# Two-model transformer kernel: three norms' squares summed on VectorE, even attention's scores in pairs over four banks

## Time and profile before

| | |
|---|---|
| median of three runs | 2680.15 us (2676.91 to 2689.09) |
| the profiled execution | 2677.15 us, its span 2675.3 us |
| TensorE, busy share of the span | 94% |
| TensorE, weight loads | 70% |
| VectorE | 44% |
| ScalarE | 18% |
| GpSimd | 9% |
| mean granted TensorE clock | 0.982 of full |
| DMA, mean | 291 GB/s |
| chain of work that ended last | TensorE 80%, DMA 12%, VectorE 6%, ScalarE 1% |

### The profile page before, as it was taken

The page is one execution under the profiler, slowest core; times in us unless marked ns, Lnnn a source line. Parts: engine busy times, 40 slices in busy tenths (PEclk is TensorE's granted clock), DMA queues, the critical chain, the costliest instruction groups (busy, mean ns, idle before and its releaser), DMA issues.

```text
span 2675.3 us, 40698 instructions
## 1 busy us (share of the span) xinstructions
PE 2523.6 (94%) x16446; PEld 1860.0 (70%) x16446; DVE 1164.0 (44%) x2714; ACT 480.5 (18%) x1041; POOL 245.2 (9%) x280
## 2 busy tenths in 40 slices
PE   6999999989989998999999799999999999999998
PEld 3555545566667964666676456679899866798997
DVE  2355114321115653111111322668777626687776
ACT  2142003221101022010000121431200114312001
POOL 0000000000001100000011000002122100021221
PEclk9999999999999999999999899999999999999999
DMA  9868999999998768999999983424644544245440
GB/s 405 342 275 360 420 413 407 418 420 393 418 419 345 312 277 337 419 418 419 418 416 416 420 346 112 144 95 158 252 160 182 209 159 146 95 158 220 158 158 17
DMA packets 121785, 779.78 MB, mean 291 GB/s; under 512 B 13248, under 2 KB 16960, under 8 KB 37888
## 3 DMA queue, kind: packets, MB, share of 16 engines
q1 hardware_dynamic: 94976, 684.76, 63.5%
q0 software_dynamic: 22560, 82.32, 8.0%
q10 hardware_dynamic: 4064, 10.09, 1.0%
HBM read 771.35 MB, written 5.77 MB: 290 GB/s over the span
## 4 chain that ended last, share of the span: by engine, by line
PE 80%; DMA 12%; DVE 6%; ACT 1%; issue 1%; SPq 0%; ACTq 0%; DVEq 0%
PE bank L758 78%; DMA ring<-in_stream 11%; PE bank L1202 1%; DMA work<-in_stream 1%; PE bank L762 1%; DVE work L2487 1%; DVE MX L2467 1%; DVE bank L2469 0%; DVE work L2380 0%; SPq L608 0%; DVE X L2421 0%; ACT work L1892 0%; ACT work L1792 0%; DVE X L2980 0%; ACT work L1788 0%
## 5 line engine op out<-in xcount | busy, mean ns | idle before, releaser
L758 PE MATMUL bank<-A,work 128*128 128x128 f32 (+1 forms) x3152 | 547.9, 323 | 8.9 <-DMA work<-in_stream 4.5
L758 PEld LDWEIGHTS bank<-A,work 128*128 128x128 f32 x3152 | 477.8, 192 | 68.2 <-issue 31.2
L758 PE MATMUL bank<-A,ring 128*128 128x128 f32 (+1 forms) x3088 | 474.9, 303 | 10.9 <-ACT A L1902 5.8
L758 PEld LDWEIGHTS bank<-A,ring 128*128 128x128 f32 x3088 | 424.5, 193 | 42.9 <-issue 12.7
L758 PE MATMUL bank<-work 128*128 128x128 f32 (+2 forms) x2704 | 398.8, 316 | 22.4 <-ACT work L1792 8.0
L758 PE MATMUL bank<-ring,A 128*32 128x512 f32 (+3 forms) x2272 | 366.4, 611 | 32.3 <-DMA ring<-in_stream 30.6
L758 PEld LDWEIGHTS bank<-work 128*128 128x128 f32 (+1 forms) x2704 | 316.8, 175 | 81.9 <-issue 38.1
L758 PEld LDWEIGHTS bank<-ring,A 128*32 128x32 f32 (+2 forms) x2272 | 116.7, 124 | 261.1 <-issue 200.8
L758 PE MATMUL bank<-work,ring 128*128 128x128 f32 (+1 forms) x1696 | 289.5, 318 | 1.6 <-DVE work L2500 1.6
L758 PEld LDWEIGHTS bank<-work,ring 128*128 128x128 f32 x1696 | 255.9, 191 | 20.2 <-DVE work L2500 2.1
L698 POOL TENSOR_TENSOR work<-ring,work 128x512 f32<-128x512 f32 (+1 forms) x106 | 141.3, 1333 | 683.2 <-DVE work L2514 546.1
(11 more groups left out here) (344 smaller groups left out, 2006.8 us busy)
## 6 DMA issues: line engine op xcount, KB each, us to landing
ring<-in_stream SPq DMA_DIRECT2D x652, 1024.0 KB, 14.9
work<-in_stream POOLq DMA_DIRECT2D x140, 512.0 KB, 9.1
spill<-work ACTq DMA_DIRECT2D x6, 512.0 KB, 6.1
work<-in_stream POOLq DMA_DIRECT2D x8, 384.0 KB, 8.5
work<-spill POOLq DMA_DIRECT2D x6, 512.0 KB, 4.7
X<-in_xt ACTq DMA_DIRECT2D x1, 2048.0 KB, 13.3
work<-spill POOLq DMA_DIRECT2D x2, 768.0 KB, 11.8
tab_sb<-in_tab_a ACTq DMA_DIRECT2D x1, 1120.0 KB, 9.5
```

The source lines that it names most:

```text
L758: return pay(pe.matmul(o, w, x, start=start, stop=stop, tile_position=place), tells)
```

## The change

1. The squares of n2_0, n1_1 and n2_1: ScalarE writes all eight chunks into buffers of their own, with no wait for TensorE. VectorE adds them, seven additions chained by a semaphore (`add_own`), in n2_0 and n2_1 one step behind the residual additions, in n1_1 behind the expert stage. TensorE makes one product of the sum with the ones (`total_square`): for n2_0 behind the first of the three strips, for n1_1 behind a context step, for n2_1 behind the first of two router strips.
2. The even attention makes two heads' scores together, over four banks (0, 1, 2, 7). The order of the heads in memory changes so that neighbouring heads lie in different halves of the partitions: the queries' weight columns were laid out as (0,4), (1,5), (2,6), (3,7) before, and head h now reads pair h // 2, half h % 2; the rows of `w_out_even` and the sinks follow the same order.
3. Its six strips of modulation rows stand at t = 1, 2, 3, 4, 6, 8. They add up in bank 6 in place of bank 2; VectorE copies that bank inside the attention loop, at t = 10, and TensorE waits for this copy before the first value product of block 1.
4. The copy for the next group (`mod_copy(3)`) moves behind the scaling of n2_0.
5. Slot n1_1 gets one context step and slot a9 loses one. VectorE's share of slot n1_1 stands behind the second weight sums of odd_in.
6. Ahead of the second router TensorE waits for the context's `out` 5 in place of 3.

```diff
@@ CONTEXT_STEPS @@
-    "c8": 2, "d8": 3, "n1_1b": 1, "a9": 2, "b9": 2, "c9": 2, "d9": 1,
+    "c8": 2, "d8": 3, "n1_1": 1, "n1_1b": 1, "a9": 1, "b9": 2, "c9": 2, "d9": 1,
...
+ATT_MOD_AT = (1, 2, 3, 4, 6, 8)
...
+SUMMED = ("n2_0", "n1_1", "n2_1")
...
+        SQUARES = {"n2_0": wk(0, KD, T), "n1_1": wk(0, KD, T), "n2_1": wk(13312, KD, T)}
+        SQUARE_SUM = wk(16128, T)
...
-        MOD_BANK = (4, 6, 2, 5, 4, 6, 5, 4, 4, 4)
+        MOD_BANK = (4, 6, 6, 5, 4, 6, 5, 4, 4, 4)
...
-        SBANKS = {"even": (0, 1), ...
+        SBANKS = {"even": (0, 1, 2, 7), ...
@@ tensor @@
+            def total_square(name):
+
+                pe.wait_ge(own_added, (KD - 1) * (SUMMED.index(name) + 1))
+                mm(bank[6][:, 0:T], ones, SQUARE_SUM, True, True, tells=True).then_inc(own_total, 1)
...
-                    pair = 2 if name[:2] == "na" else 1
+                    pair = 1 if name[:3] == "mla" else 2
...
                             elif u0:
                                 pe.wait_ge(at_p, u0)
+                            elif i == SBANKS[name].index(7):
+                                pe.wait_ge(mod_taken, 3)
...
-                    filling = name == "even" and 1 <= t <= EVEN_OUT_MOD - ATT_MOD
-                    if filling:
-                        mod_rows(ATT_MOD + t - 1)
+                    if name == "even" and t in ATT_MOD_AT:
+                        mod_rows(ATT_MOD + ATT_MOD_AT.index(t))
...
                         pe.wait_ge(at_ptc, g + 1)
+                        if h == 1 and name == "even" and b == 1:
+                            pe.wait_ge(mod_copied, 3)
...
-                      lambda h, b: QK[64 * (h // 4):64 * (h // 4) + 64, h % 4, b * P:(b + 1) * P],
-                      lambda h: KV_K[64 * (h // 4):64 * (h // 4) + 64, :],
-                      lambda kb, h: V1[:, kb, 64 * (h // 4):64 * (h // 4) + 64],
+                      lambda h, b: QK[64 * (h % 2):64 * (h % 2) + 64, h // 2, b * P:(b + 1) * P],
+                      lambda h: KV_K[64 * (h % 2):64 * (h % 2) + 64, :],
+                      lambda kb, h: V1[:, kb, 64 * (h % 2):64 * (h % 2) + 64],
...
-            for n in range(EVEN_OUT_MOD, ROUTE_MOD[0]):
+            mod_rows(EVEN_OUT_MOD)
+            total_square("n2_0")
+            for n in range(EVEN_OUT_MOD + 1, ROUTE_MOD[0]):
                 mod_rows(n)
-            norm("n2_0", T)
...
             beside("n1_1")
-            norm("n1_1", T)
+            total_square("n1_1")
             beside("n1_1b")
...
-            norm("n2_1", T)
-            wait_ctx(pe, "out", 3)
-            route_mods(1, 0, 2)
+            wait_ctx(pe, "out", 5)
+            route_mods(1, 0, 1)
+            total_square("n2_1")
+            route_mods(1, 1, 2)
@@ scalar @@
+            def own_squares(name, come):
+
+                i = SUMMED.index(name)
+                act.activation(OPEN[:, :], EPS[:, 0:1], ACT.Sqrt)
+                for k in range(KD):
+                    come(k)
+                    act.activation(SQUARES[name][:, k, :], X[:, k, 0:T], ACT.Square).then_inc(own_square, 1)
+                act.wait_ge(own_total, i + 1)
+                act.activation(RSTD, bank[6][:, 0:T], ACT.Sqrt, bias=EPS[:, 0:1], scale=1.0 / D).then_inc(std_ready, 1)
...
-                squares(name, w, lambda k: X[:, k, 0:w], come=come)
+                own_squares(name, come)
@@ vector @@
+            def add_own(name, k):
+
+                i = SUMMED.index(name)
+                dve.wait_ge(own_square, KD * i + k + 1)
+                if k > 1:
+                    dve.wait_ge(own_added, (KD - 1) * i + k - 1)
+                dve.tensor_tensor(SQUARE_SUM, SQUARES[name][:, 0, :] if k == 1 else SQUARE_SUM, SQUARES[name][:, k, :], ALU.add)\
+                   .then_inc(own_added, 1)
...
                         normalize(t - 1)
+                    if name == "even" and t == HEADS + 2:
+                        dve.wait_ge(mod_raw, 3)
+                        mod_copy(2)
...
-            dve.wait_ge(mod_raw, 3)
-            mod_copy(2)
             take_mods(2, 0, 2, 0, 6)
...
+                for k in range(1, 3) if j == 3 else range(j - 1, j) if j > 3 else ():
+                    add_own("n2_0", k)
+            add_own("n2_0", KD - 1)
...
             norm("n2_0", T, ...
+            dve.wait_ge(mod_raw, 4)
+            mod_copy(3)
...
-            beside("n1_1")
+            for k in range(1, KD):
+                add_own("n1_1", k)
             link(gain(3, 1, 8, 0, par_("g1", KD, KD)))
             sum_weights(-1, 0)
...
             sum_weights(-1, 1)
+            beside("n1_1")
             beside("n1_1b")
...
                 residual("odd_out", j, T, MOD[:, 1, 16 + j, 0:1])
+                if j > 1:
+                    add_own("n2_1", j - 1)
+            add_own("n2_1", KD - 1)
```

More of the change, by code:

```diff
@@ L174 @@
     NBASE[_n], NSTAT[_n], NMEAN[_n], NOUT[_n], NMID[_n], NXC[_n] = _b, _s, _m, _o, _d, _x
-    _b += 0 if _n in SHIFTED else NCHUNK[_n]
+    _b += 0 if _n in SHIFTED + SUMMED else NCHUNK[_n]
     _d += 0 if _n == "final" else NCHUNK[_n]
@@ L454, in build_program @@
         odd_sums = sem("odd_sums")
+        own_square, own_added, own_total = sem("own_square"), sem("own_added"), sem("own_total")
         ffn_scalar, ffn_vector = sem("ffn_scalar"), sem("ffn_vector")
@@ L486, in build_program @@
         UNIT0 = {"na": 0, "mla0": 8, "mla1": 12}
-        SBANKS = {"even": (0, 1), "na0": (0, 1, 2, 7), "mla0": (0, 1, 2), "na1": (0, 1, 2, 7), "mla1": (0, 1, 2)}
+        SBANKS = {"even": (0, 1, 2, 7), "na0": (0, 1, 2, 7), "mla0": (0, 1, 2), "na1": (0, 1, 2, 7), "mla1": (0, 1, 2)}
         def score_bank(name, g):
@@ L2660, in _ @@
                     beside("in_d")
-            dve.wait_ge(mod_raw, 4)
-            mod_copy(3)
+                for k in range(1, 3) if j == 3 else range(j - 1, j) if j > 3 else ():
+                    add_own("n2_0", k)
+            add_own("n2_0", KD - 1)
             def over_pass(q, p, g2):
@@ L3223, in lay_out @@
                  _tm(w[:, 1280:1792]), _pad(16)])
-    put("even_out", [_fm(I["w_out_even"][0])])
+    put("even_out", [_fm(I["w_out_even"][0][np.r_[order, 512:D]])])
     for l in range(2):
@@ L3286, in lay_out @@
         p(a, _vec(I[b]))
-    p("sink", np.broadcast_to(I["attn_sink"].reshape(1, HEADS), (P, HEADS)))
+    p("sink", np.broadcast_to(I["attn_sink"].reshape(2, 4).T.reshape(1, HEADS), (P, HEADS)))
     rb = np.stack([np.concatenate([I["b_router_group"][l], I["b_router_expert"][l]]) for l in range(2)])
```

## The result

The changed kernel took 2660.26 us (median of four runs, 2658.59 to 2661.65), the kernel before 2680.82 in the same comparison; the ratio on record is 0.9931, with a 95% interval of 0.9906 to 0.9956 (the two medians alone give 0.9923). That is 20.6 us less, where 12.3 had been forecast, and inside the range given (2658 to 2676). Two later comparisons gave 18.3 us (ratio 0.9935) and 15.9 us (0.9941). Over all of the runs the medians are 2678.7 (43 runs of the kernel before, 2669.4 to 2689.1) and 2660.6 (15 runs of the changed one, 2656.9 to 2663.0): 18.1 us.

The account below looks back on a forecast made before the run. TensorE was taken to set the pace up to 208 us, the weight stream from there. Gains of 8.7 + 0 + 1.2 + 2.4 = 12.3 us against the midpoint 2678.65 gave 2666.4 us, range 2658 to 2676.

Parts of the forecast that it names:

- Attention: Even attention: paired scores and the early copy start even_out at 170.2 instead of 178.89, a gain of 8.7 us.
- The first part: Even attention up to the scores of heads 10 and 11, bound by TensorE: 27.5 us from 124.53, ending at 152.0.
- VectorE's part: Even attention from 152.0 on, bound by VectorE's tops, normalizations and copies: 14.3 us, ending at 166.3.
- the tail of 2.9 us: End of the even attention: last normalization to last value product stays 2.9 us, ending at 169.2.
- the case "1.7 more": Even attention: if the half-clock stretch, seen at the first strip, goes, 1.7 us more are gained.
- The clock rival: Rival: clock falls where VectorE bounds the attention and TensorE idles between pieces; 10.7 us lost, 2677.1; chance 0.07.
- n2_0, 0 forecast: First norm: path 4.3 us shorter, but waited out in the second unit's 18.82 us ring wait; 0 taken, ends 0 and 4.3.
- The ring wait in the second unit longer, by some 4 us: Sign, second unit of the first expert stage: the wait for the ring grows by some 4 us.
- n1_1 and a9: Second norm: TensorE goes on about 2.3 us later, a context step moved out of a9 gives 3.5; gain 1.2.
- the step is not won back: Rival in a9: that expert unit waits for its weights anyway, so +3.5 us, 2669.9; chance 0.10.
- n2_1: Third norm: one product puts the root 2.4 us earlier, and the router waits for it; gain 2.4, ends 0.7 and 4.
- Slower: Rival, first expert stage: context steps 4.3 us out of step with the stream, nine units lose 38.7, 2705.1; chance 0.05.

Follow-up runs that it names:

- n2_0 old with the late copy: The changed kernel with n2_0 as eight products again, the copy of modulation rows still behind its scaling; 2662.31 us.
- attention alone: The kernel before with only the changed kernel's even attention, all norms and context steps as before; 2666.66 us, ratio 0.9961.
- attention with n2_0: The changed kernel with n1_1, n2_1 and the context steps as before; 2664.69 us.
- the norms alone: The changed kernel with the old even attention, one head's scores at a time over two banks; 2670.88 us, ratio 0.9977.

## Why the prediction held, and where its steps failed

**Attention, 8.7 forecast, 8.5 to 10.2 measured** in the eight traces with this attention. The first part was to end at 152.0 and the next piece starts at 151.55; VectorE's part was to take 14.3 us and ends at 165.90, 14.3 later; the tail of 2.9 us and the start of even_out right behind the columns came as worked out. In the first trace the first strip took 2.85 us in place of 3.62, as only part of it ran at the lower clock. The trace in which all of it did (3.62, n2_0 old with the late copy) has the lead of 8.5, and the three in which that stretch is missing (0.97 becomes 1.00 in the window of 120 to 172 us) have 10.1 to 10.2: the case "1.7 more" of the prediction, to the tenth. The Trainium skill's "TensorEngine Tiling (Array Packing)", under PSUM Bottleneck, warns that emptying the banks may come to bound what packed products give. The trace agrees for half of it: 7.8 of VectorE's 14.4 idle microseconds went, and behind head 10 VectorE is the bound, with TensorE waiting 0.24 to 1.30 us for its normalizations.

**The clock rival** did not come true there. The pair at 154.34 took 1.13 us amid those waits, and the granted clock from 150 to 170 us is 1.00 in every trace. The rule named for it (the Trainium skill, "TensorE: Matmul & The Clock Gate", under HAM oscillation) is not borne out at this place by any trace here; its own example has a wait for DMA behind each burst of products, so this place is no full test of it. Ahead of the first router the traces lean its way: in the two where TensorE waits 2.87 and 2.86 us for a late copy, all of the router's 32 products behind it ran at the lower clock and took 7.02 us; in the twelve others they took 3.74 to 5.74.

**n2_0, 0 forecast; nothing left in the path behind the second unit, 1.8 to 2.9 us in the medians.** The value was right for the stream, and the reasoning had a hole: "the chain waits 18.82 us for the ring" was taken for room in which any gain is waited out. The room was 1.01 + 2.72 us, less than the 4.2 won. So the 0 was in part luck. Between the router and the end of the second unit the changed kernel loses 4.9 us of its lead, more than n2_0 had given: 1.65 in the new wait at 224.57, 0.8 in the two ring waits of the unit, and most of the rest to the lower clock (1.1 in the router's products, 5.19 + 3.65 us against 4.31 + 3.41, and 0.5 in the products between the ring waits, 5.34 against 4.82). In all, ring waits between 208 and 830 us, the new one included, are 12.5 us against 10.5. "The ring wait in the second unit longer, by some 4 us" was wrong: the chain's piece grew by 1.5 us and TensorE's own waits by 0.8. Behind the second unit the four traces with the new n2_0 and the same stream lead by 8.4 to 9.8 us, the four with the old one by 9.4 to 11.5. The 1.8 us between the medians of the one set that has both kernels has overlapping ranges; the 2.9 us is taken over sets (2660.6 and 2663.5).

**n1_1 and a9, +1.2 forecast, +1.3 measured in the first trace:** -2.1 and +3.5. The +3.5 is in all ten traces with the edit. The loss is 2.1 in seven of them and 3.6 to 5.2 in three, where the products around the sum ran at the lower clock (0.83 to 0.91 from 812 to 832 us, 1.00 in all the others), so the mean of the ten is +0.7. The two other traces without the edit (attention alone, and attention with n2_0) have no loss there, and they and both of the kernel before have the whole clock; whether the new wait of 2.65 us brings the lower clock on is not shown by three of ten against none of four. The rival "the step is not won back" falls. The addition chained at 0.53 us and the start behind the overflow branch were right. One figure of the working is off: 834.2 less today's 832.25 is 2.0 us, not 2.3.

**n2_1, +2.4 forecast, +2.2 measured.**

**The sum** was therefore right at its places (12.8 against 12.3) and short against the medians, by 5.8 of 18.1 us. The base was right too: "I set the sum against the midpoint", 2678.65, and the 43 runs of the kernel before have a median of 2678.7. What failed is the step from the sum to the whole: it took everything between the four places as unchanged, and 5.3 us more than the steps explain went there. The attention alone has 1.3 such microseconds over its step and the norms alone 2.9 over theirs. Three things on record bear on them.

- Between the second unit and n1_1 the changed kernel's three traces win 2.3, 1.7 and 3.0 us over the first trace of before, but the second trace of before wins 3.3 there, so this may be the course of the one trace that all leads are read against.
- Behind a9, where no edit stands, the ten traces with the new n1_1 and n2_1 win -1.8 to 4.2 us, 2.0 in the mean (the changed kernel 4.2, 4.1 and 2.1), and the three without win -2.5 to -0.3. The means point at the norms, the single traces overlap.
- Each run has its mean granted clock on record. Over the 39 runs of the kernel before in the three later sets, 0.001 less clock goes with 1.9 us more (correlation -0.76), over the norms alone with 1.7 (-0.94), over the 15 runs of the changed kernel with 0.8 (-0.58). The mean clocks are 0.9807 before and 0.9816 changed, so by these slopes 0.7 to 1.7 us of the difference go with the clock, an estimate from a correlation and not a cause shown.

Which coupling of ring, context quarters and clock gives the rest was not settled. That the measured time lies inside the range is owed to its lower end of 2658, which was made of n2_0 counting in full and the half clock gone; neither is what the traces show as the cause, so that is in part luck.

**Slower** (the first expert stage out of step with the stream, 38.7 us) did not happen in any version, even with the router 13 us earlier.

**Of faster, same and slower** 0.53 was given to "same" within 0.5%, 0.42 to faster. The medians differ by 0.77%, and the interval of the ratio is 0.44 to 0.94%: faster, and most likely beyond the 0.5%, so the larger chance stood on the wrong side.

## What to carry to other kernels

A piece of a chain of waits that names a transfer is that transfer's time, not the engine's idle time; before calling a gain swallowed, read in the engine's own timeline how long it really stood. Where a ring feeds the kernel, ask what is in its slots while the stream stands: moving weights that are used early ahead of those used late, without any less work, was worth another 10 us here on top of the change's 15.9 in the same set. And compare several executions before a sum of steps is set against one of them: here two profiles of one kernel differ by 3.4 us, as much as the largest of the three steps behind the first expert stage.

## What the runs showed of the hardware that was not expected

The kernels with the old attention scatter more from run to run than those with the new one. The kernel before ranged over 13, 16 and 11 us in the three sets with their 11 to 17 runs and the norms alone over 12 in twelve runs; the changed kernel ranged over 3, 5 and 6 us, its variants over 3 to 9, in four to six runs each. That more runs range wider is only a part of it: the standard deviation, which does not grow with the number of runs, is 4.1 us over the 39 later runs of the kernel before and 4.4 over the norms alone, against 2.0 over the 15 of the changed kernel and 1.1 to 3.2 for its variants. The granted clock ranges alike (0.977 to 0.984 before, 0.978 to 0.984 changed), but the same difference of clock goes with twice the time in the kernels with the old attention. Why was not tried.

The stretches of half clock come back at the same work in most executions of one program, and a few move. The three traces of the changed kernel have 17, 15 and 19 of them, and twelve stand at the same products in all three: from 210 to 218 us the mean clock is 0.57 in each, from 575 to 580 us 0.66, from 954 to 962 us 0.57, 0.57 and 0.56. Between 1034 and 1040 us, on the other hand, they were granted 1.00, 0.81 and 0.50. The two traces of the kernel before have 0.68 and 0.97 in that window, but there it is one stretch of 6.8 us at the same work, which begins at 1031.0 in the one and, 3.5 us of lead on, at 1027.5 in the other. One stretch moved the lead of all that follows by 1.3 to 2.1 us in the second trace of the kernel before, as much as n2_1 is worth.
